# Bias mask in GpSimd pieces behind the preparation, gate rows awaited by their reader, and a fused bias and maximum for the neighbourhood heads

## What is computed

```python
bias = rel_bias[:, dr + (NA_WIN_ROWS - 1), dc + (NA_WIN_COLS - 1)]
s_nb = q_row . k_nb * scale + bias          # 8 x 16 neighbours of a token
s_c  = q_row . k_ctx * scale                # 256 context keys
p = softmax(concatenate([s_nb, s_c]))
...
x  = x + g1 * (concatenate([a_lat, b_lat, c_lat, d_lat]) @ w_out[l])
h2 = modulate(rms_norm(x, norm_ffn[l]), sh2, sc2)
x  = x + g2 * moe_ffn(h2, ...)
```

## Time and profile before

| | |
|---|---|
| median of 3 runs | 2052.8 us (2051.13 to 2060.31) |
| profiled execution, whole / its span | 2054.72 us / 2052.9 us |
| TensorE busy | 1693.2 us, 82% of the span |
| VectorE, ScalarE, GpSimd busy | 903.8, 424.3, 284.6 us |
| chain that ended last | PE 67%, DMA 10%, DVE 9%, issue 8%, SPq 4%, ACT 1%, POOL 1% |
| mean granted TensorE clock | 0.911 of full speed |

### The profile page before, as it was taken

How to read it: one execution, slowest core, us unless ns; L and a number is a source line. 1 busy time by engine, 2 the same in 40 slices (tenths; PEclk the granted TensorE clock), 3 DMA queues, 4 the chain that set the end, 5 groups by cost and what they waited for, 6 DMA issues and landing times.

```text
span 2052.9 us, 22977 instructions
## 1 busy us (share of the span) xinstructions
PE 1693.2 (82%) x7934; PEld 1026.0 (50%) x7934; DVE 903.8 (44%) x1852; ACT 424.3 (21%) x878; POOL 284.6 (14%) x332
## 2 busy tenths in 40 slices
...
GB/s 254 332 170 11 77 23 174 184 1 32 32 11 52 208 237 200 154 270 321 336 346 336 273 246 11 19 2 195 164 1 32 32 28 179 77 292 322 342 339 163
DMA packets 157876, 332.42 MB, mean 162 GB/s; under 512 B 32461, under 2 KB 91019, under 8 KB 143635
## 3 DMA queue, kind: packets, MB, share of 16 engines
...
...
## 4 chain that ended last, share of the span: by engine, by line
PE 67%; DMA 10%; DVE 9%; issue 8%; SPq 4%; ACT 1%; POOL 1%; DVEq 0%; POOLq 0%; ACTq 0%
PE S L1215 14%; PE S L1031 11%; PE S L1232 7%; PE S L1091 7%; PE B L1156 7%; PE PT L1108 4%; PE B L1139 4%; PE B L1031 3%; DMA arena<-in_w_in 3%; DMA arena<-in_w_mod 2%; DMA arena<-in_moe_w_down 2%; DMA arena<-mod 2%; DVE nmax L1694 1%; DMA arena<-y,arena 1%; PE S L979 1%
## 5 line engine op out<-in xcount | busy, mean ns | idle before, releaser
L1215 PE MATMUL S<-arena 128*128 128x256 f32 x1472 | 335.3, 387 | 7.1 <-DMA arena<-in_moe_w_down 5.0
L1215 PEld LDWEIGHTS S<-arena 128*128 128x128 f32 x1472 | 283.6, 194 | 65.1 <-issue 26.3
L1031 PE MATMUL S<-arena 128*128 128x480 f32 x640 | 278.7, 581 | 10.0 <-DMA arena<-in_w_in 6.7
L809 ACT ACTIVATE arena<-S,nmax 128x768 f32<-128x768 f32 (+1 forms) x200 | 161.8, 812 | 200.2 <-DVE nmax L1694 200.2
L1694 DVE TENSOR_REDUCE nmax<-S 128x1 f32<-128x768 f32 (+1 forms) x200 | 163.7, 846 | 88.8 <-PE S L1091 74.4
L1091 PE MATMUL S<-arena 64*128 64x256 f32 (+5 forms) x720 | 170.8, 527 | 33.7 <-ACT arena L809 32.0
L1031 PEld LDWEIGHTS S<-arena 128*128 128x128 f32 x640 | 120.2, 195 | 134.0 <-issue 119.4
L1232 PE MATMUL S<-arena 128*128 128x512 f32 x368 | 171.8, 607 | 5.0 <-DVE arena L1794 2.1
L1156 PE MATMUL B<-arena 128*128 128x512 f32 x320 | 156.7, 619 | 2.5 <-DVE arena L1747 1.8
L1108 PE MATMUL PT<-cst,arena 128*128 128x128 f32 x832 | 125.3, 284 | 28.6 <-ACT arena L809 18.5
L1108 PEld LDWEIGHTS PT<-cst,arena 128*128 128x128 f32 x832 | 96.1, 144 | 90.8 <-issue 60.9
...
## 6 DMA issues: line engine op xcount, KB each, us to landing
...
y<-arena SPq DMA_DIRECT2D x36, 512.0 KB, 10.3
...
```

The lines of the kernel that those rows point to most:

```text
L809: act.activation(p_buffer(k, m)[:, 0:nk], (S0, S1)[m][:, 0:nk], ACT.Exp, bias=nmax[:, 2 * k + m:2 * k + m + 1], accum_out=rsum[:, 2 * k + ...
L1031: mm = pe.matmul(ubank[c][:, 0:UCH], hT[b][:, k, :], win[:, k, c * UCH:(c + 1) * UCH], start=k == 0, stop=k == KT - 1)
L1215: mm = pe.matmul(G[:, 512 * w:512 * w + DE], X[:, k, :], wk, start=k == 0, stop=k == KT - 1)
```

## The change

- SyncE: `s_first_loads` waits for all scores (`scored`) instead of all values (`pv_done`); the wait for `pv_done` comes behind the shared expert's three weights, and the router's weights behind that wait.
- ScalarE: `x1_square` of the last tile moves from the end of the attention loop behind `first_T` of the shared expert (layer 0) or behind `ffn` of block 0 (layer 1). The loop over blocks is written out.
- TensorE: tile 0's transposes come ahead of the waits for `s_w_in` and `res_mul`.
- GpSimd: the mask waits for the last preparation round (`round_evac`) and is added in eight pieces of 512 columns, each with its own signal; the wait for `vec_in` moves into `x1_h2`.
- VectorE: the lambda steps up to `lam_sum` move ahead of `prep(T - 1)`; the waits for `round_evac` and `vec_in` ahead of the step loop go, the latter into `gated`; the wait for the next layer's modulation rows moves into `mod_row`. A neighbourhood map now takes a maximum over the 256 context columns, a fused `tensor_tensor_reduce` that adds the bias, writes the scores back and carries the maximum on, and a one-column multiplication by -1. A map waits for the pieces of its own head alone.

```diff
--- before.py
+++ after.py
@@ -599,13 +599,14 @@
                 def s_first_loads():
 
 
-                    sp.wait_ge(s["pv_done"], NJ * gend)
+                    sp.wait_ge(s["scored"], 2 * NS * gend)
                     for b in range(2):
                         s_load(b, b, True)
-                    sp.dma_start(rw, A["router_w"].rearrange("(p k) n -> p k n", k=KT)).then_inc(s["s_w_in"], 16)
                     for name, e0 in (("shared_w_gate", 0), ("shared_w_up", DE)):
                         sp.dma_start(swgu[:, :, e0:e0 + DE], A[name][l].rearrange("(p k) n -> p k n", k=KT)).then_inc(s["s_w_in"], 16)
                     sp.dma_start(swd, A["shared_w_down"][l].rearrange("(p k) n -> p k n", k=2)).then_inc(s["s_w_in"], 16)
+                    sp.wait_ge(s["pv_done"], NJ * gend)
+                    sp.dma_start(rw, A["router_w"].rearrange("(p k) n -> p k n", k=KT)).then_inc(s["s_w_in"], 16)
                     sp.dma_start(rb, A["router_b"].partition_broadcast(P)).then_inc(s["s_w_in"], 16)
                     for stream in range(2):
                         sp.dma_start(g2[:, stream, :], mod_d[l][stream, 5 * D:6 * D].partition_broadcast(P)).then_inc(s["s_w_in"], 16)
@@ -851,8 +852,6 @@
                         out_product(*divmod(n - 1, NS))
                     if t >= 2 and k == 0:
                         x1_square(t - 2)
-                x1_square(nt - 1)
-                nt = T if l == 0 else TL
                 gend = T * l + nt
 
                 def ffn(m, gi, b, more):
@@ -868,11 +867,12 @@
                     act.activation((hT2, XT)[m == "e_"][b][:, 4:8, :].rearrange("p a b -> p (a b)"), PT[:, 512:1024], ACT.Copy).then_inc(s[m + "t_s"], 1)
 
                 first_T("s_", g(0), 0)
-                with act.Fori(0, nt // 2 - 1) as i:
-                    for b in range(2):
-                        ffn("s_", g(2 * i + b), b, True)
-                ffn("s_", g(nt - 2), 0, True)
-                ffn("s_", g(nt - 1), 1, False)
+                for t in range(nt):
+                    if l == 0 and t == 0:
+                        x1_square(nt - 1)
+                    ffn("s_", g(t), t % 2, t < nt - 1)
+                    if l and t == 0:
+                        x1_square(nt - 1)
 
                 act.wait_ge(s["s_lg"], gend)
                 act.activation(score[:, 0:nt, :], lg[:, 0:nt, :], ACT.Exp, scale=-1.0).then_inc(s["r_exp"], 1)
@@ -1233,9 +1233,6 @@
                     mm.then_inc(s[m + "d"], 1)
 
 
-                pe.wait_ge(s["res_mul"], 2 * gend)
-                pe.wait_ge(s["s_w_in"], 16 * 7 * (l + 1))
-
                 def s_next(t, b, first, half):
                     if half == 0:
                         pe.wait_ge(s[f"hs_in{b}"], hs_count(t, b))
@@ -1250,6 +1247,8 @@
 
                 for half in range(2):
                     s_next(0, 0, l == 0, half)
+                pe.wait_ge(s["s_w_in"], 16 * 7 * (l + 1))
+                pe.wait_ge(s["res_mul"], 2 * gend)
                 def s_block(t, b, more, first):
                     if not first:
 
@@ -1378,10 +1377,11 @@
 
                 pool.wait_ge(s["bias_in"], 16 * 8 * (l + 1))
 
-                bt = bias_t.rearrange("p h (j c) -> p (h j) c", c=GRID_W)
-
-                pool.wait_ge(s["r8_ready"], T * (l + 1))
-                pool.tensor_tensor(bt, bt, C("window").unsqueeze(1).to_broadcast([P, 64, GRID_W]), ALU.add).then_inc(s["bias_ready"], 1)
+                pool.wait_ge(s["round_evac"], ROUNDS * T * (l + 1))
+                for h in range(4):
+                    for half in range(2):
+                        bt = bias_t[:, h, 512 * half:512 * half + 512].rearrange("p (j c) -> p j c", c=GRID_W)
+                        pool.tensor_tensor(bt, bt, C("window").unsqueeze(1).to_broadcast([P, 8, GRID_W]), ALU.add).then_inc(s["bias_ready"], 1)
 
                 def diff_rstd(t, c):
                     pool.wait_ge(s["d_stat"], FINALS * g(t) + c + 1)
@@ -1394,6 +1394,7 @@
                     gp = g(t)
                     w = 0 if t < TL else 3
                     ch = Count(pool, s["g_x"], 4 * gp)
+                    pool.wait_ge(s["vec_in"], 16 * 6 * (l + 1))
                     pool.wait_ge(s["xa_in"], 16 * gp + 16)
                     pool.wait_ge(s["res_mul"], 2 * gp + 2)
                     pool.tensor_tensor(xb, xb, xa, ALU.add).then_inc(s["x1_ready"], 1)
@@ -1405,7 +1406,6 @@
                     pool.tensor_tensor(h2b, h2b, vec[:, w + 2, :], ALU.add).then_inc(s["h2_ready"], 1)
                     assert ch.n == 4
 
-                pool.wait_ge(s["vec_in"], 16 * 6 * (l + 1))
                 nt = tiles_of(l)
                 for t in range(nt):
                     if t >= 2:
@@ -1510,6 +1510,8 @@
                     dve.tensor_copy(mod_bufs[l][1][b], bank).then_inc(s["mod_part"], 1)
 
                 def mod_row(l, n, bank):
+                    if l and n == 0:
+                        dve.wait_ge(s["mod_rows_in"], 16 * 12)
                     dve.wait_ge(s["mod_sel"], n + 1 + NMCH * l)
                     row = mod_bufs[l][2][:, span(n * MCH, MCH)]
                     dve.tensor_tensor(row, bank[0:2, :], row, ALU.add).then_inc(s["mod_row"], 1)
@@ -1657,8 +1659,6 @@
                     prep(t)
                     normalise(l, t + 2)
                 prep(T - 2)
-                prep(T - 1)
-
 
                 nt = T if l == 0 else TL
                 gend = T * l + nt
@@ -1670,6 +1670,7 @@
                 ch.done(dve.tensor_scalar(subg[:, :], subg[:, :], 1.0 - lam_init, None, ALU.mult))
                 ch.sync()
                 dve.sem_inc(s["lam_sum"], 1)
+                prep(T - 1)
                 dve.wait_ge(s["lam_exp"], l + 1)
 
                 ch.done(dve.tensor_tensor(nlam[:, 2:3], nlam[:, 1:2], nlam[:, 0:1], ALU.subtract)).sync()
@@ -1687,11 +1688,15 @@
                             dve.scalar_tensor_tensor(dvar[:, c, :], dvar[:, c, :], EPS, S0[:, NTOK:NTOK + 2], ALU.mult, ALU.add).then_inc(s["d_stat"], 1)
                         if kind == "n" and nk == NTOK:
                             if n == NS * g(0) + k:
-                                dve.wait_ge(s["bias_ready"], l + 1)
-
-                            bt = bias_t[:, 2 * h + m:2 * h + m + 1, (7 - 2 * t) * GRID_W:(7 - 2 * t) * GRID_W + SEQ]
-                            att_ch.done(dve.tensor_tensor(Sm[:, 0:SEQ].unsqueeze(1), Sm[:, 0:SEQ].unsqueeze(1), bt, ALU.add)).sync()
-                        dve.tensor_reduce(nmax[:, 2 * k + m:2 * k + m + 1], Sm[:, 0:nk], AX.X, ALU.max, negate=True).then_inc(s["neg_max"], 1)
+                                dve.wait_ge(s["bias_ready"], 8 * l + 4 * h + 2 * m + 2)
+
+                            bt = bias_t[:, 2 * h + m, (7 - 2 * t) * GRID_W:(7 - 2 * t) * GRID_W + SEQ]
+                            over_ctx, over_all = dtmp[:, 2 * m:2 * m + 1], dtmp[:, 2 * m + 1:2 * m + 2]
+                            att_ch.done(dve.tensor_reduce(over_ctx, Sm[:, SEQ:nk], AX.X, ALU.max)).sync()
+                            att_ch.done(dve.tensor_tensor_reduce(Sm[:, 0:SEQ], Sm[:, 0:SEQ], bt, 1.0, over_ctx, ALU.add, ALU.max, over_all)).sync()
+                            dve.tensor_scalar(nmax[:, 2 * k + m:2 * k + m + 1], over_all, -1.0, None, ALU.mult).then_inc(s["neg_max"], 1)
+                        else:
+                            dve.tensor_reduce(nmax[:, 2 * k + m:2 * k + m + 1], Sm[:, 0:nk], AX.X, ALU.max, negate=True).then_inc(s["neg_max"], 1)
 
                 def out_heads(t, job):
 
@@ -1743,14 +1748,13 @@
 
                         dve.wait_ge(s["x1_stored"], 16 * g(t))
                         dve.wait_ge(s["h2_ready"], g(t))
+                    dve.wait_ge(s["vec_in"], 16 * 6 * (l + 1))
                     dve.wait_ge(s["op_mm"], 2 * g(t) + c + 1)
                     dve.tensor_tensor(xb[:, c * 512:(c + 1) * 512], B7[:, :], vec[:, 0 if t < TL else 3, c * 512:(c + 1) * 512],
                                       ALU.mult).then_inc(s["res_mul"], 1)
 
                 if l == 0:
                     att_ch = Count(dve, s["v_o"], 0)
-                dve.wait_ge(s["round_evac"], ROUNDS * T * (l + 1))
-                dve.wait_ge(s["vec_in"], 16 * 6 * (l + 1))
                 for n in range(NS * nt + 3):
                     t, k = divmod(n, NS)
                     if t >= 2 and k == 0:
@@ -1814,8 +1818,6 @@
                     dve.tensor_tensor(ob[b], (S0, S1)[b][:, :], g2[:, stream, :], ALU.mult).then_inc(s["s_ob"], 1)
 
                 first_T("s_", g(0), 0)
-                if l == 0:
-                    dve.wait_ge(s["mod_rows_in"], 16 * 12)
                 for b in range(2):
                     s_block(b, 0, b, True, l == 0, 0)
                 if l == 0:
```

## The result

The changed kernel takes 2038.5 us (median of 5 runs, 2029.1 to 2046.8), beside 2058.8 us (5 runs, 2051.1 to 2066.9) for the kernel before in the same comparison: a ratio of 0.990, 95% interval 0.986 to 0.995. Against the 2052.8 us from which the forecast started, the median of the first three of those five, it is 14 us lower, in its own comparison 20 us lower. So the change is worth 15 to 20 us, about 0.8 to 1.0%.

A forecast was written before the change was run, and what follows sets the result against it. TensorE was taken to lead the chain that ended last, so parts pay only where it waits. -9.5 - 9.1 + 0.6 - 2.4 - 2.4 + 3.6 = -19.2 us, from 2052.8 to 2033.6 us; forecast 2029 to 2039, range 2023 to 2044.

The forecast's parts named there:

- collision: Tile 0: mask pieces hold the first differential step's ratio and combination; +0.6 for both layers, ceiling 2.2 per layer.
- openings: Start of each layer's attention: first maxima no longer wait for `vec_in`, nor layer 1's copy for the mask; -9.5 and -9.1.
- Rival E: Openings wait for something hidden behind `vec_in`, so only one of them is won: 2043 us, chance 0.07.
- neighbourhood steps: Attention: the fused map form gains 0.6 per step, four steps in tile 0, -2.4; no gain from the other 12.
- Rival D: Neighbourhood maps: the fused operation is slow; the change loses from a 1.75 us form, 2061 at p = 1.3; chance 0.04.
- 1.4 either way: Both openings: a step running at TensorE's full clock level earlier or later is worth 1.4 us in each layer.
- SyncE's loads: Shared expert's first loads: they stand behind the wait for `h2_stored`, so replacing `pv_done` by `scored` changes 0.
- Rival A: Shared expert: the loads come earlier after all, as `pv_done` was the wait that ends last: 2018 us, chance 0.05.
- part 4: TensorE's transposes ahead of both shared-expert waits: router product 2.7 us earlier in either layer; -2.4 taken for layer 0.
- new wait in layer 1: Shared expert, block 1: the late square delays tile 2's load, TensorE waits 5 us; with clock, +3.6 net.
- Rival B: Layer 1's shared expert: the load of tile 2 arrives in time, -2.7 instead of +3.6: 2027 us, chance 0.15.
- Rival C: The openings give back 10.6 us through collisions, lost warm-up steps and a slower fused form: 2044 us, chance 0.12.

The follow-up runs named there:

- first profile: The changed kernel profiled after the change: 2038.5 us median of 5 runs against 2058.8 for the kernel before; the profiled execution was the fastest, 2029.1.
- second profile: The changed kernel once more with no edit, profiled with the experiments: 2042.4 us (6 runs, 2033.2 to 2043.5).
- second comparison: The changed kernel against the kernel before, measured again for the experiments: 2042.4 us against 2057.4, ratio 0.992 (0.990 to 0.993).
- part 4 alone taken away: The changed kernel with TensorE's transposes again behind the two waits of the shared expert, everything else as changed: 2059.4 us.

## Why the prediction was right, point by point

The forecast was 2033.6 us, from 2052.8, so -19.2. Measured: -20.4 and -15.0 in two comparisons. The stages that the change touches sum to -16.7 in the first profile and -16.3 in the second. The median itself, 2038.5 us, is 4.9 above the forecast and just inside 2029 to 2039; two more runs of the kernel before raised its own median by 6.0.

| step | predicted | measured, first / second profile |
|---|---|---|
| opening of layer 0 | -9.5 | -9.45 / -9.45 |
| opening of layer 1 | -9.1 | -9.03 / -9.03 |
| tile 0, both layers: collision +0.6, steps -2.4, clock not counted | -1.8 | +0.60 / -0.10 |
| layer 0: transposes ahead, to block 5 | -2.4 | -1.18 / -1.01 |
| layer 1: transposes ahead, square late, to block 3 | +3.6 | +2.38 / +3.25 |
| all | -19.2 | -16.7 / -16.3 |

That -20.4 lies so near to -19.2 is luck: the stages fell short of the sum by 2.5 and 2.9 us, and what lies beyond them in the -20.4 isn't shown to be the change's doing; the second comparison has -15.0. The mechanism of the two openings, 18.5 of the 19.2, was right; the step that wasn't is tile 0, where -1.8 was forecast and +0.6 and -0.1 measured.

**The openings** came out of subtraction within 0.1 us. The row that carried them was the one with the releaser: `mod` for VectorE, where its work needed only the scores, and those rows land no earlier now. Rival E (one opening only, 2043) falls with the two first maxima. Removing the mask from beside the copy did all that was said, and the experiments show that place or size would each have done for the copy.

**The collision** was real, and 0.43 and 0.48 us where I took 0.3 per layer: the two holds sum to 2.0 and the scores cover three quarters of it. What remains is seen twice in after: TensorE idle 0.59 us for L1738 (359.41; no such wait where the mask stands elsewhere), and the second maxima late, since VectorE is in order and they stand behind the held combination. The combination ended 2.0 us late in both layers, and "over 1 us late" was named as a sign that the prediction is wrong: the hold was nearly its ceiling of 2.2, and the cover by the scores is what kept the price small. The pieces took 10.53 us instead of 8.80: they start 1.22 us apart and not 1.1, and the last was held for 0.7.

**The neighbourhood steps** gave 0.43 and not 0.6 each, because the accumulator's read is an instruction of its own (0.14 us) and the fused form took 0.76 rather than 0.70. That is near the fast one of the bounds 0.70 and 1.18, and together 0.7 us less than forecast. Rival D needed 1.75 us in one form. That later tiles gain nothing was right.

**Tile 0's clock** is what the sum left open. The third scores of layer 0 in before, and in after:

```profile
370.92 1.56 PE L1091 MATMUL S<-arena 32*128 32x512 f32 x8 [1.51 <-ACT arena L809]
```

```profile
362.19 2.93 PE L1091 MATMUL S<-arena 32*128 32x512 f32 x8 [1.23 <-ACT arena L810]
```

The windows of after, from the first maximum to the end of the fourth step and from there to tile 1:

```profile
core 0: us, PE busy (x) PEld busy (x) DVE busy (x) ACT busy (x) POOL busy (x), PEclk, DMA share, GB/s
353.00:376.50 23.50, 16.14 (x74) 9.52 (x74) 14.46 (x26) 9.29 (x19) 7.49 (x6) 0.57 1.04 338
376.50:415.20 38.70, 31.64 (x277) 22.26 (x277) 24.26 (x50) 20.17 (x39) 1.99 (x4) 1.00 0.38 108
```

And the same two of before:

```profile
362.10:384.10 22.00, 13.93 (x73) 8.43 (x73) 13.02 (x21) 9.22 (x19) 0.00 (x0) 0.68 1.05 303
384.10:425.90 41.80, 34.80 (x277) 24.52 (x278) 24.76 (x46) 20.32 (x39) 1.98 (x4) 0.92 0.14 42
```

From the first maximum to the fourth step it takes 1.50 us more than before, and four terms make it up: the collision +0.43, one neighbourhood step -0.43, the third scores +1.37 (2.93 us at the low level, 1.2 GHz, where in the timeline of before they take 1.56 at the full 2.4), the fourth +0.13 (2.93 for 2.80). The granted clock of the stretch fell from 0.68 to 0.57. Behind it the clock is full where it was 0.92, and TensorE's busy time falls by 3.16. So the "1.4 either way" for a step at the other level was the right size for one such step; there were several, of both signs, and together they moved tile 0 by +1.4 us in the first profile and +0.7 in the second, both layers added (+0.60 and -0.10 less the -0.8 that collision and steps explain). Which steps they are differs between profiles of the same code, and what decides it stays open. The end of layer 1's attention has one more, which earns nothing: the last stage before the shared expert is 1.35 us shorter, because the last value product (L1139) takes 1.53 us and not 2.73. With the mask at its old place it takes 2.67, and the stage is as long as before, but the router product starts 39.8 us behind the end of attention in both: it waits for the gate rows.

**SyncE's loads** stayed where they were, as said: the old wait put back changes nothing. Rival A falls by the profile itself. That the place in the queue held the loads is confirmed by the experiment that issues them a tile earlier.

**TensorE's order** in layer 0 gave 2.73 at the router product, and what block 5 keeps of it is 1.0 to 1.2. In the first profile the wait for the weights ends 0.2 later behind the end of attention than before, and waits of 0.24 for `in_w_mod` and of 0.59 and 0.49 for `h` take most of the rest. In the second profile it is the clock: the gate and up products of block 0 (L1215) take 10.02 us, 8.85 in the first profile, 8.73 before and 7.15 in later blocks. A value near the upper bound of the gain was taken, with a row at hand (weights asked for only behind `h2_stored`) that spoke for less. A link was missing here, too: the square "goes behind the first transposed copy, which is now over before the square could start: nothing" holds only with part 4, and the working didn't say so. Priced one by one, the parts gave 2.7 and 0. With part 4 alone taken away, the stretch is 12 to 13 us longer. In layer 1 the router product came 2.9 us earlier, about as forecast.

**The new wait in layer 1** was right in every link. Only its size was off: 4.27 us instead of 5, because the load took 4.2 us and not 4.9, and the clock's share: the transposes took 1.11 us instead of 0.71 and the down product 4.22 instead of 3.70, so 0.9 and not 1.4. Rival B (no wait) and its reason, that the load might be faster than 4.9, were half right: it was faster by 0.7 us, and that removes a wait of 0.7, not one of 5.

**Rival C** (the openings give back 10.6 us) had three parts. Beyond what I took the collision cost 0.3 of its 3.8, the clock 0.7 to 1.4 of its 2.8, the fused form 0.7 of its 4.0.
